# Order of the loads of the dense expert stage, and sixteen gathered rows placed between the table batches

## What is computed

```
s1, i1 = top_k(scores with 128 keys of half 0, 16);  s2, i2 = the same for half 1
top_s, pos = top_k(s1[:, None] + s2[None, :], 16)        # per token and head
idx = i1 * 128 + i2;  gates = softmax(top_s)             # 8 heads x 16 = 128 experts a token
act = gelu(einsum('tkd,td->tk', expert_u[idx], xf))
out = h + einsum('tk,tkd->td', gates * act, expert_v[idx])
```

## Time and profile before

| | |
|---|---|
| median of three runs | 2559.58 us (2558.06, 2559.58, 2563.25) |
| the profiled execution | 2563.25 us, its span 2561.5 us |
| PE busy | 2475.5 us, 97% of the span |
| DVE busy | 1972.3 us, 77% |
| POOL busy | 1466.3 us, 57% |
| ACT busy | 424.1 us, 17% |
| DMA | 857.68 MB, mean 335 GB/s |

### The profile page before, as it was taken

One profiled execution on the slowest core, in us unless ns is written; L12 is line 12 of the kernel. 1 busy time (PEld: TensorE's weight loads), 2 busy tenths in 40 slices (PEclk: granted clock), 3 DMA queues, 4 the chain that ended last, 5 costly groups with the idle time before them and its releaser, 6 DMA issues.

```text
span 2561.5 us, 24119 instructions
## 1 busy us (share of the span) xinstructions
PE 2475.5 (97%) x7561; PEld 1363.3 (53%) x7561; DVE 1972.3 (77%) x4252; ACT 424.1 (17%) x782; POOL 1466.3 (57%) x1169
## 2 busy tenths in 40 slices
PE   8999999998888899999999999999999999999998
PEld 6687776876766344444444444444444444444443
DVE  4308888787778788777898777779787777988877
ACT  0213213221887000110010000000000000000001
POOL 0000487577600267666666767667676776766664
PEclk9999999998999999999999999999999999999999
DMA  8544886865666899979999999999999999999997
GB/s 321 221 162 163 313 289 181 328 206 132 187 192 196 335 352 387 403 284 387 390 419 390 390 388 399 387 419 419 420 401 391 415 386 413 416 416 410 413 410 263
DMA packets 288063, 857.68 MB, mean 335 GB/s; under 512 B 42048, under 2 KB 99392, under 8 KB 273344
## 3 DMA queue, kind: packets, MB, share of 16 engines
q0 software_dynamic: 167184, 541.73, 55.2%
q1 hardware_dynamic: 108400, 289.25, 30.0%
q10 hardware_dynamic: 12352, 25.17, 2.6%
HBM read 807.75 MB, written 48.30 MB: 334 GB/s over the span
## 4 chain that ended last, share of the span: by engine, by line
PE 87%; DVE 4%; ACT 4%; DMA 2%; issue 1%; DVEq 1%; ACTq 0%; SPq 0%
PE pairs L827 34%; PE pairs L781 33%; PE pairs L695 15%; ACT arena L981 2%; PE pairs L738 1%; PE pairs L713 1%; DMA arena<-in_w_all 1%; PE pairs L794 1%; ACT arena L1005 1%; PE pairs L765 1%; DMA arena<-gate_tables 1%; DMA gate_tables<-arena 1%; ACT arena L983 0%; ACT pick_all L860 0%; ACTq L982 0%
## 5 line engine op out<-in xcount | busy, mean ns | idle before, releaser
L675 POOL DMA_INDIRECT ring<-in_expert_u,idx x512 | 667.0, 1303 | 614.6 <-DVE dots L1182 349.3
L827 PE MATMUL pairs<-arena 128*128 128x512 f32 x2048 | 883.5, 593 | 6.9 <-DVE arena L1248 6.2
L781 PE MATMUL pairs<-arena 128*128 128x512 f32 x2048 | 882.5, 592 | 0.0
L675 POOL DMA_INDIRECT ring<-in_expert_v,idx x512 | 583.0, 1139 | 278.5 <-issue 120.8
L1182 DVE CUSTOM_DVE_ANT_0 junk<-ring,xf 128x1024 bf16<-128x1024 f32 x512 | 610.3, 1224 | 156.2 <-DMA ring<-in_expert_u,idx 152.4
L827 PEld LDWEIGHTS pairs<-arena 128*128 128x128 f32 x2048 | 390.1, 191 | 498.0 <-issue 497.5
L781 PEld LDWEIGHTS pairs<-arena 128*128 128x128 f32 x2048 | 388.9, 190 | 486.1 <-issue 486.1
L1193 DVE SCALAR_TENSOR_TENSOR arena<-ring,arena 128x1024 f32<-128x1024 f32 x381 | 473.4, 1283 | 78.7 <-DMA ring<-in_expert_v,idx 76.5
L695 PE MATMUL pairs<-arena 128*128 128x256 f32 (+1 forms) x1792 | 401.1, 387 | 10.2 <-DMA arena<-in_w_all 5.0
L695 PEld LDWEIGHTS pairs<-arena 128*128 128x128 f32 x1792 | 346.9, 194 | 62.5 <-issue 6.7
L989 ACT ACTIVATE arena<-pairs 128x512 f32<-128x512 f32 x128 | 76.4, 597 | 1167.3 <-PE pairs L781 1167.2
(11 more groups left out here) (174 smaller groups left out, 1085.1 us busy)
## 6 DMA issues: line engine op xcount, KB each, us to landing
arena<-in_w_all SPq DMA_DIRECT2D x80, 1024.0 KB, 6.3
arena<-in_uT SPq DMA_DIRECT2D x128, 512.0 KB, 6.8
arena<-in_expert_v SPq DMA_DIRECT2D x128, 512.0 KB, 8.9
arena<-gate_tables SPq DMA_DIRECT2D x32, 1024.0 KB, 11.0
gate_tables<-arena SPq DMA_DIRECT2D x11, 2048.0 KB, 9.1
gate_tables<-junk ACTq DMA_DIRECT2D x4, 2048.0 KB, 14.8
ring<-in_expert_u,idx POOLq DMA_INDIRECT x512, 8.9
ring<-in_expert_v,idx POOLq DMA_INDIRECT x512, 8.8
```

What stands on the lines that cost most here:

```text
L675: nc.gpsimd.indirect_dma_start(out=ring[:, r % RING, :], out_offset=None, in_=expert_u if table == "u" else expert_v, in_offset=bass.Indir ...
L781: last = nc.tensor.matmul(score_bank[x], uslot[:, x % USLOTS, k * P:(k + 1) * P], xfT[:, k, :], start=(k == 0), stop=(k == KD - 1))
L827: last = nc.tensor.matmul(o_bank[n % 4], gated[:, x % GSLOTS, t * P:(t + 1) * P], vrows[:, j, half * 512:(half + 1) * 512], start=(j == 0) ...
```

## The change

`HOT_FILL` goes from 0 to 1.0. `take(1.0)` gives one row (its planned cost is 1.35), so one gathered row is now placed behind each of the batches 2, 5, 8, ..., 47: rows 64 to 79. They leave `late`, and the places of the later units of DVE shift a little. SP's loads of the dense stage are written as a loop over the same list of tiles and pieces that PE follows, in another order.

```
-HOT_FILL = 0.0
+HOT_FILL = 1.0
...
-            assert next_u == EARLY
-            load_gates(2)
-            for g in range(GROUPS):
-                tiles = list(range(VJ * (g + 1) + 2, min(VJ * (g + 2) + 2, KEYS)))
-                for x, sums_done in zip(tiles, (1, 2, 4, 5)):
-                    sp.wait_ge(o_full, SUMS * g + sums_done)
-                    load_u(x)
-                    if sums_done == 2:
-                        load_gates(2 * g + 3)
-                if g + 1 < GROUPS:
-                    load_v(g + 1, 0)
-                    load_v(g + 1, 1)
-                for i, x in enumerate(tiles[:USLOTS + 1]):
-                    if x + USLOTS in tiles:
-                        load_u(x + USLOTS)
-                    sp.wait_ge(s_full, x + 1)
-                    load_v(g + 1, 2 + i)
-                    if i == USLOTS:
-                        load_v(g + 1, 3 + i)
-                    if i == 2 and 2 * g + 4 < HALF_GROUPS:
-                        load_gates(2 * g + 4)
+            while next_u < EARLY + USLOTS:
+                load_u(next_u)
+                next_u += 1
+            pending = []
+            for kind, a, b in dense:
+                if kind == "tile":
+                    if EARLY <= a < KEYS - USLOTS:
+                        load_u(a + USLOTS)
+                    if pending:
+                        load_v(*pending.pop(0))
+                    if a % GJ == 0 and 0 < a and a // GJ + 1 < HALF_GROUPS:
+                        load_gates(a // GJ + 1)
+                elif b == SUMS - 1 and a + 1 < GROUPS:
+                    for j in range(3):
+                        load_v(a + 1, j)
+                    pending = [(a + 1, j) for j in range(3, VJ)]
```

## The result

The changed kernel is slower: 2582.1 us at the median of its four timed runs (2580.3 to 2588.5) against 2561.4 before on the same chip (four runs). The ratio is 1.0086 with a 95% interval of 1.0066 to 1.0104. That is 20.7 us more by the medians and 22.0 by the ratio, where I had forecast 11.4 more and a range up to 2580. The profiled execution is slower than any of the timed ones: 2591.2 us, span 2589.5, which is 28.0 above the profiled one of before. So its losses in the dense stage are to be read as places, not as the sizes of a typical run.

What follows compares the result with a forecast made beforehand. PE was taken to bound the dense stage and ACT the table batches. Terms of 9.6, 0.2, 0.3 and 1.0 us made 11.1 us on top of the median 2559.58, so 2571 us, range 2564 to 2580.

Steps and rivals of the forecast that it cites:

- What bounds the kernel: Dense stage: PE sets the time, so earlier loads or lighter DVE win nothing beyond 6.9 us; table batches: ACT sets the pace.
- PE follows PE: Chain of waits from 862.53 us on: PE waits only for itself, 54.93 us a stage.
- Part 1: Rows 64 to 79 among the table batches: DVE waits for row 65's late gather; 9.6 us lost, plus 0.2 later.
- Row 65's wait: Table batches: DVE stands 12.5 us because gather 65, issued behind the last scatter, lands only at 691.4.
- The later cycles: Table batches after the second scored tile: rows fit into DVE's idle of 5.30 us; 0.2 us, bounds 0 and 13.7.
- Part 2: Dense stage's start: third gate load, behind four key loads, lands 5.1 us later; 0.3 us, bounds 0 and 5.
- Part 3: Each dense group: SP's loads, all in the tile stage, displace six gathered rows; 1 us for all groups, bounds 0 and 8.
- It catches up in the piece stage, where SP's queue is now empty: Dense groups: DVE, up to 10.8 us further behind after the tiles, is 3.6 to 7 us behind by the second sum.
- Once PE has waited, the margins behind it have grown: Dense stage: argument against losses in several groups, given margins of 3.3, 4.1 and 8.3 us.
- the dense stage pays as well: Rival, 13 in 100: the burst of loads costs its full shift in one group, 7 to 8 us on top, 2578.
- The clock: After PE's idle in the batches, half clock without added loss; rival, 5 in 100: it reaches a scored tile, 2578.

Runs made afterwards that it cites:

- e2: The changed kernel with HOT_FILL back at 0, so the new order of loads alone; 2582.3 us, ratio 1.0082.
- e13: e2 with every fourth gather from row 128 on replaced by a plain load of the same size on POOL; 2565.0 us, ratio 1.0009.
- e1: The kernel before with HOT_FILL at 1.0, so the rows among the batches alone with the old order of loads; 2569.1 us, ratio 1.0037.
- e14: The changed kernel with the key loads from tile 16 on cut to half their columns; 2571.2 us, ratio 1.0038.
- e9: e2 with the third gate load put back ahead of the four key loads at the dense stage's start; 2586.1 us, ratio 1.0085.
- e7: e2 with the key loads from tile 16 on cut to half their columns; 2561.2 us, ratio 1.0006.

## Why the prediction was wrong

**What bounds the kernel.** Right in the main: PE sets the dense stage, and it lost where it waited. But "PE follows PE" in the chain hid how near the next bound is. A group has some 63 rows to gather (634 in groups 3 to 12). In the piece stages of these ten groups POOL issued 346 of them before, 340 in e2 and 356 in e13: between losing 21 us and 2 lie 1.6 rows a stage, and before, with no loss at all, lies between the two. So the count alone doesn't decide; when the rows come does.

**Part 1, the rows.** Right at each step. Row 65's wait was 12.27 us (12.5 worked out), PE's 7.18 (7.2), the loss by the second scored tile 9.6 (9.6), alone 9.5 us by the clock (e1), and 9.7 with the rest neutralised (e14). The later cycles cost nothing (I had 0.2). "DVE has 16 rows less in this stage, which helps a little" was right and too modest for e1, where DVE's lag is 3 to 7 us lower in nine of the sixteen groups.

**Part 2, the third gate load.** I took 0.3 us with bounds of 0 and 5. e9 shows no gain from putting it back, so nothing contradicts the size, though e9's spread is too wide to confirm it; e7's 1.6 us of PE at group 0 are within the bounds. Group 0 took 3.3 us longer than before in the changed kernel, but 2.7 of them show in e1 too, which has the old order.

**Part 3, the loads in each group: the step that failed.** I took 1 us with bounds of 0 and 8; it measured 21 us alone and, by the changed kernel's 20.7 to 22 less the 9.6 of part 1, 11 to 12 beside the rows. The first half of the step held in kind and was twice too large: SP's loads in a full tile stage displace gathers, but these loads grew by 1.57 MB and not by 3.15, and DVE gets through about three rows fewer there and not six (263 against 288 in the ten tile stages of groups 3 to 12 in e2, 257 in the changed kernel). What failed is the sentence "It catches up in the piece stage, where SP's queue is now empty". It catches up too little: at the last sum of groups 7, 10 and 11 the changed kernel's lag is still 16 to 19 us, where before it was 1 to 5. The queue isn't empty (1.57 MB), and a shorter SP queue helps little, because POOL's issue of gathers is near its own limit there. Two stretches of 11 us in the second half of e2's piece stage of group 7 (columns as in the earlier trace rows; POOL's busy time and count are the fifth pair):

```profile
1657.00:1668.00 11.00, 11.00 (x27) 4.87 (x26) 10.70 (x20) 0.00 (x0) 9.08 (x7) 1.00 0.91 332
1668.00:1679.00 11.00, 11.00 (x27) 4.82 (x26) 9.53 (x17) 0.00 (x0) 8.87 (x8) 1.00 0.89 309
```

and the same place before:

```profile
1652.00:1663.00 11.00, 11.00 (x27) 4.79 (x26) 8.75 (x15) 0.00 (x0) 8.07 (x8) 1.00 1.03 421
1663.00:1674.00 11.00, 11.00 (x27) 4.91 (x26) 9.48 (x17) 0.00 (x0) 8.79 (x9) 1.00 1.02 419
```

With gathers alone the DMA moves 309 to 332 GB/s: POOL issues 7 or 8 in 11 us and is busy but for the 0.3 us between two of them. Before, SP's loads filled the difference to 420. The change moved them to where the DMA was full and left that room empty. How much of the lag hangs on this limit, and how much on the fuller tile stages alone, no run separates: e13 relieved both.

From this follow two more errors. I priced each group by itself, against its own margin; the lag is handed on, from group 6 to 7 to 8 and from 10 to 11 to 12, as the lags at the last sums show. "Once PE has waited, the margins behind it have grown" is not so: a wait of 1.64 us in group 7 was followed by one of 3.33 in group 8. And I watched the sums only, where 11.8 of the 12.9 us behind group 0 end with the gate product of a group's last tile, whose margin I never worked out: it was 4.3 us in group 3 and 7.8 to 8.4 in groups 7, 8 and 12 before, and the lag grew by 6 to 12 in these and in group 11.

**The rivals.** The nearest was "the dense stage pays as well", at 13 in 100 and 7 to 8 us; it is what happened, at 11 to 12. Its price was the one shift of one group. The range ended at 2580 for the same reason: I had bounded the term by one group's miss. Of the 11 us between the forecast and the measured time, 1.8 are the median of before, which was 2559.6 when I forecast and is 2561.4 over the four runs here.

**The clock.** The two longest waits behind group 0 cost more than their length, because PE then ran at half speed for a few us (5.6 us lost for 3.33 waited, 5.8 for 4.04). I had that in the earlier trace rows and used it only for a rival.

## What to carry to other kernels

Moving a load out of a stretch where it seems to crowd is only free if something else can use the room; ask what limits the other stream there, and count its issue time on its own engine, gaps included. Where an engine off the critical path gets its data with little to spare over a whole period, price a change by what it does to the whole period and let the lag carry from one period to the next, for every product that the critical engine waits for. For a wait that an instruction takes on in an in-order engine, the arithmetic of landing time less arrival is reliable to tenths of a us: 12.27 against 12.5, and 7.18 against 7.2, here.

## What the hardware showed that I had not expected

POOL's issue of a gather of 0.524 MB depends on what DVE does: 1392 ns each in a piece stage with DVE busy 46.6 of 55 us, 962 ns with DVE's row products halved and DVE busy 33.2. From 1000 to 2500 us of e2 a gather takes between 932 and 1992 ns; the longest exceed the shortest by 1.06 us, less than one of DVE's row products (1223 ns; 692 when halved). The gathers that e13 issued while a row product ran took 1363 ns on average, the others 986. A plain load of the same size takes POOL 0.58 us, and DVE doesn't lengthen it: e13's 215 plain loads took 562 to 606 ns each, 47 of them wholly within one row product.

The Trainium skill, "SBUF — State Buffer", section "SBUF: two separate sides", tells of one pair of ports that DVE and GpSimd share under an exclusive lock, held for a whole instruction; whichever comes second is blocked. A DVE operation with two SBUF inputs takes part in this only against a GpSimd operation that reads SBUF. DVE's row products have two such inputs; a gather reads its row numbers (`idx`) there, and a plain load has none to read. By that rule a gather would be lengthened by up to one DVE instruction and a plain load not at all, and the durations above agree. Two gathers fall out of this: one of 3019 ns in e13 and one of 3050 ns in the changed kernel exceed the shortest by 2.1 us. That it is this lock, no run here shows by itself.
